# Spreading the four row pairs of the mLSTM mixer over 64 partitions each: selector products on TensorE, or transfers within on-chip memory

## The reference

```python
a_inter = fcum + m0f[:, None, :]
m_t = jnp.maximum(a_inter, jnp.max(dmat, axis=2))
wmat = jnp.exp(dmat - m_t[:, :, None, :])
s = jnp.einsum('bthd,bshd->btsh', qf, kf) * wmat
inter = jnp.exp(a_inter - m_t)
num = inter[..., None] * jnp.einsum('bthd,bhde->bthe', qf, c0f) + jnp.einsum('btsh,bshe->bthe', s, vf)
den = inter * jnp.einsum('bthd,bhd->bth', qf, n0f) + jnp.sum(s, axis=2)
h = num / jnp.maximum(jnp.abs(den), jnp.exp(-m_t))[..., None]
```

## Time and profile before

| | |
|---|---|
| median of 3 runs | 3158.34 us (3158.18 to 3158.46) |
| the profiled execution's own time | 3152.57 us |
| its span, first to last instruction | 3150.7 us |
| mean granted clock of TensorE | 0.947 of full speed |
| TensorE busy | 2927.8 us (93%) |
| VectorE, ScalarE, GpSimd busy | 1327.5, 1120.5, 1446.1 us (42, 36, 46%) |
| mean DMA rate | 83 GB/s |

### The profile page before, as it was taken

The page is one execution under the profiler, slowest core; times in us unless marked ns, Lnnn a source line. Parts: engine busy times, 40 slices in busy tenths (PEclk is TensorE's granted clock), DMA queues, the critical chain, the costliest instruction groups (busy, mean ns, idle before and its releaser), DMA issues.

```text
span 3150.7 us, 43886 instructions
## 1 busy us (share of the span) xinstructions
PE 2927.8 (93%) x18104; PEld 2543.3 (81%) x18104; DVE 1327.5 (42%) x2341; ACT 1120.5 (36%) x1734; POOL 1446.1 (46%) x912
## 2 busy tenths in 40 slices
PE   4768879999999999999999989999999999999998
PEld 3556568787887789898997888778788778999998
DVE  6444246435532455453442344743653242222222
ACT  4322154332332344443223244443233233322222
POOL 2143144345652474445653364434564246455554
PEclk9878689999998999999999999999999899999999
DMA  2111022322221242222222124222222124222332
GB/s 106 39 35 42 25 88 75 94 89 87 81 82 54 83 147 88 88 81 78 83 82 74 55 94 128 88 75 94 87 81 82 49 88 148 88 94 94 90 96 84
DMA packets 80292, 261.26 MB, mean 83 GB/s; under 512 B 10722, under 2 KB 12002, under 8 KB 80096
## 3 DMA queue, kind: packets, MB, share of 16 engines
q1 hardware_dynamic: 63008, 228.04, 23.1%
q10 hardware_dynamic: 17088, 30.43, 2.7%
HBM read 244.90 MB, written 13.54 MB: 82 GB/s over the span
## 4 chain that ended last, share of the span: by engine, by line
PE 81%; DVE 9%; ACT 3%; POOL 3%; issue 2%; ACTq 1%; DMA 1%; SPq 0%; DVEq 0%; POOLq 0%
PE pj L500 23%; PE pj L502 23%; PE pj L501 23%; DVE sl L1482 2%; PE pm L574 2%; PE pm L744 2%; PE pm L838 1%; PE pm L843 1%; POOL w_lo L1371 1%; PE pm L816 1%; PE pm L812 1%; POOL m_lo L1455 1%; DVE sl L1628 1%; ACT w_hi L896 1%; DVE wide L1894 1%
## 5 line engine op out<-in xcount | busy, mean ns | idle before, releaser
L1371 POOL TENSOR_TENSOR w_lo<-w_raw,w_hi 128x1024 fp32r<-128x1024 f32 x428 | 1047.0, 2450 | 1047.2 <-ACT w_hi L896 1047.1
L500 PE MATMUL pj<-hid,w_hi 128*128 128x260 f32 (+1 forms) x1920 | 630.4, 328 | 26.9 <-POOL hid L1448 13.0
L500 PE MATMUL pj<-m_hi,w_hi 128*128 128x260 f32 (+1 forms) x1920 | 623.0, 325 | 10.3 <-POOL m_lo L1455 5.8
L502 PE MATMUL pj<-hid,w_lo 128*128 128x260 f32 (+1 forms) x1920 | 620.7, 323 | 0.0
L502 PE MATMUL pj<-m_hi,w_lo 128*128 128x260 f32 (+1 forms) x1920 | 615.2, 320 | 0.0
L501 PE MATMUL pj<-m_lo,w_hi 128*128 128x260 f32 (+1 forms) x1920 | 614.4, 320 | 0.0
L896 ACT ACTIVATE w_hi<-w_raw 128x1024 fp32r<-128x1024 f32 x428 | 448.4, 1051 | 442.1 <-PE pj L502 408.9
L501 PE MATMUL pj<-hid,w_hi 128*128 128x260 f32 (+1 forms) x1536 | 495.4, 323 | 0.0
L500 PE MATMUL pj<-n_hi,w_hi 128*128 128x260 f32 (+1 forms) x1200 | 395.4, 329 | 30.8 <-DVE n_lo L1523 30.2
L1482 DVE TENSOR_TENSOR res<-res,pj 128x260 f32<-128x260 f32 (+1 forms) x432 | 219.2, 512 | 473.4 <-PE pj L502 471.9
L500 PEld LDWEIGHTS pj<-hid,w_hi 128*128 128x128 f32 x1920 | 367.3, 191 | 62.8 <-POOL hid L1448 14.3
(11 more groups left out here) (298 smaller groups left out, 3483.3 us busy)
## 6 DMA issues: line engine op xcount, KB each, us to landing
w_raw<-in_w SPq DMA_DIRECT2D x428, 512.0 KB, 3.5
out_y<-res ACTq DMA_DIRECT2D x16, 260.0 KB, 4.6
out_y<-res ACTq DMA_DIRECT2D x16, 256.0 KB, 4.6
sl<-in_x ACTq DMA_DIRECT2D x4, 520.0 KB, 5.4
res<-in_x ACTq DMA_DIRECT2D x8, 260.0 KB, 4.8
res<-out_y ACTq DMA_DIRECT2D x8, 260.0 KB, 5.0
res<-in_x SPq DMA_DIRECT2D x4, 512.0 KB, 6.6
res<-out_y ACTq DMA_DIRECT2D x8, 256.0 KB, 4.9
```

The source lines that it names most:

```text
L500: pe.matmul(out, wh, hi[:, k, c0:c1], start=(k == 0), stop=False)
L502: last = pe.matmul(out, wl, hi[:, k, c0:c1], start=False, stop=(k == n - 1))
L1371: pool.tensor_tensor(w_lo[:, j % RAW_BUFS, :], w_raw[:, j % RAW_BUFS, :], w_hi[:, j % HI_BUFS, :].bitcast(F32), ALU.subtract).then_inc(lo_ ...
```

## The change

TensorE's selector products for n = 0 to 3 and ScalarE's copies of them go. In their place ScalarE issues, at the step n = 0 and behind the same wait for do1, eight transfers from `rows8` to `nsp`: for each of the four slots i and each half h, one row is read (a single partition, repeated 64 times) and written to 64 partitions. Their semaphore `bc_ld` reaches 128 per pass when all eight have landed. GpSimd waits for it ahead of the first `qe` of a pass, in place of its wait for the copies; VectorE waits for it ahead of the first update of the state. TensorE's own wait for the copies, ahead of L812, goes.

```diff
@@ -208,7 +208,7 @@
-            elif what in ('rope', 'rot', 'norm1', 'norm2') or what == 'mprep' and x[2] < 4:
+            elif what in ('rope', 'rot', 'norm1', 'norm2'):
...
@@ -787,15 +787,13 @@
             def mprep(x):
                 q, n = x[1:]
-                if n == 4:
-                    pe.wait_ge(hc_sv, NC * (q + 1))
...
+                if n < 4:
                     return
-                at = 64 if n < 2 else 32
-                mix(MIX[x], q, sel[at:at + 4, n % 2 * P:(n % 2 + 1) * P], rows8[at:at + 4, :])
+                pe.wait_ge(hc_sv, NC * (q + 1))
...
@@ -803,7 +801,6 @@
                     if c == 0:
-                        mixed(pe, MIX[('mprep', q, 3)] + len(TILES[q % 2]))
                         for name in ('dq0', 'dq1', 'dk0', 'dk1'):
                             evicted(pe, ('job', q, name))
...
@@ -1198,14 +1195,19 @@
                     act.wait_ge(mm, SHOT[('job', q, 'do1')] + len(TILES[q % 2]))
                     if q % 2:
                         act.dma_start(nflat(4, 2)[:, 0:1024], cs_in[q // 2]).then_inc(cs_ld, 16)
+                    act.wait_ge(rows_a, 3 * q + 3)
+                    tok = TOKENS[q % 2]
+                    for i in range(4):
+                        for h in range(2):
+                            row = (64 if i < 2 else 32) + 2 * (i % 2) + h
+                            act.dma_start(nsp[64 * h:64 * h + 64, i, 0:tok],
+                                          rows8[row:row + 1, 0:tok].unsqueeze(1).to_broadcast([1, 64, tok])).then_inc(bc_ld, 16)
...
                     act.activation(tiny[:, 0:16], pm[:, 3, 0:16], ACT.Copy).then_inc(mp_w, 1)
-                    return
-                take_mix(MIX[x], q, nsp[:, n, :], ACT.Copy)
...
@@ -1426,7 +1428,7 @@
                 if c == 0:
-                    mixed(pool, MIX[('mprep', q, 1)] + len(TILES[q % 2]))
+                    pool.wait_ge(bc_ld, 16 * 8 * (q + 1))
...
@@ -1991,6 +1993,8 @@
                 dve.wait_ge(mc_nt, 2 * g + 2)
+                if c == 0:
+                    dve.wait_ge(bc_ld, 16 * 8 * (q + 1))
```

More of the change, by code:

```diff
@@ L427, in build @@
         nm_a, nm_r, nm_v = sem("nm_a"), sem("nm_r"), sem("nm_v")
-        mp_t, mp_w = sem("mp_t"), sem("mp_w")
+        mp_t, mp_w, bc_ld = sem("mp_t"), sem("mp_w"), sem("bc_ld")
         mc_t, mc_w, mc_s, mc_k, mc_q, mc_nt, mc_d, mc_h, mc_sv = (
@@ L789, in mprep @@
                 q, n = x[1:]
-                if n == 4:
-                    pe.wait_ge(hc_sv, NC * (q + 1))
[L792 to L795, removed]
-                    return
-                at = 64 if n < 2 else 32
-                mix(MIX[x], q, sel[at:at + 4, n % 2 * P:(n % 2 + 1) * P], rows8[at:at + 4, :])
+                if n < 4:
+                    return
+                pe.wait_ge(hc_sv, NC * (q + 1))
+                for j in range(2):
+                    last = pe.matmul(pm[:, 3, j * 8:j * 8 + 8], sel[0:4, j * P:(j + 1) * P],
+                                     rows8[0:4, S0:S0 + DEC], start=True, stop=True)
+                last.then_inc(mp_t, 1)
             def mc(x):
```

## The result

The changed kernel takes 3270.98 us (median of 6 runs, 3264.26 to 3277.34) against 3157.64 us for the kernel before (6 runs): a ratio of 1.0362, with a 95% interval of 1.0346 to 1.0378. It is slower by 113 us; 127 were forecast, and the time lies within the range. The profiled execution took 3270.76 us with a span of 3269.0.

A forecast was written before the change was run, and what follows sets the result against it. TensorE, 81% of the chain, was taken to bound, bare from do1 to first readout. Gaps of 41.9 us (even) and 43.9 (odd), 171.6 in place of 44.9, gave +126.7: 3279.3 profiled, 3285 as median; range 3195 to 3350.

The forecast's parts named there:

- The bare stretch: From do1's last product to the first readout, once per pass: nothing covers it, 44.9 us in all before the change.
- The size of the transfers: Time for the eight row transfers' 1.05 MB per pass: from 2.4 us at 435 GB/s to 38.5 at 27.2 GB/s.
- the narrow end: One source partition feeds no more than one DMA engine's worth, 27.2 GB/s: 38.5 us per even pass, 39.2 odd.
- the paragraph on the port table: Trainium skill, SBUF ports: four neighbouring partitions share one port of some 27.2 GB/s; 19.3 us for each four transfers.
- The row on which the size leaned: Value-cache load into 127 partitions in odd passes, nearest by shape: 520,192 B in up to 31.5 us, at least 16.5 GB/s.
- The sum: Gaps from do1 to first readout: 41.9 us even, 43.9 odd, 171.6 in all in place of 44.9, +126.7.
- The state load's delay: Odd passes, ScalarE's queue: state load L1200 goes ahead of the transfers, 0.35 us to issue and 1.2 for its 512 KB.
- The hand-over: From the transfers' landing to the readout: 1.0 us, made of qe's 0.72 and two hand-overs.
- B: Rival at the row transfers: narrow but twice as wide, gaps 94.0 us in all, +49, 3207 us; chance 0.16.
- C: The forecast itself: narrow row transfers, likeliest 3285 us, by itself 3260 to 3350, rates down to 19 GB/s; chance 0.64.
- D: Rival at the row transfers: half a path, 13.6 GB/s, engines in each other's way, +282, 3440 us; chance 0.06.
- A: Rival at the row transfers: one partition feeds all engines, gaps 28 to 37 us in all, about 3146 us; chance 0.14.

## Why the prediction was right

*The bare stretch.* It was right that nothing covers the four places: +115.1 us of gap became +118.3 of span. The remaining 3 us are of no one place. Before do1 of the first pass, where no instruction differs, the kernel after is already 4.35 us later (334.26 against 329.91), and over the whole program such differences partly cancel. No weights came late either: what the dense products waited for split weights (L500 on `w_lo`) is 6.7 us in both kernels.

*The size of the transfers.* Here the two ends were 2.4 and 38.5 us with a factor of sixteen between, and the narrow end was chosen. It was right: 38.06 us from the first issue to qe in the first pass. The reason given was the single source partition; the two runs with other sources show that it is the source, and the pair on 32 and on 96 shows that it is a path shared by a group, not the partition, as the paragraph on the port table had it.

The row on which the size leaned hit it by luck. The load of 127 rows was near in rate, but it is narrow in another way, which the prediction had allowed for. Here is ScalarE's queue, q10 (packets, MB, share of sixteen engines), in the 12 us from 566 while that load drained before, and in the 34 us from 338 of the kernel after:

```profile
q10 hardware_dynamic: 64, 0.26, 5.7%
...
q10 hardware_dynamic: 599, 0.98, 86.9%
```

The cache load moved 22 GB/s and took 0.057 of sixteen engines, about the time of one. The row transfers moved 29 and kept fourteen engines' worth of time occupied. So the row was a good guide only because about one engine's time and one source path came to nearly the same rate.

*The sum* was too high by 11.6 us (171.6 for the gaps, 160.0 measured). Nearly all of it lies between the first issue and qe: data and fixed part were put at 40.1 us even, and at 40.8 odd with 1.2 more behind the state load; it took 38.06, 38.2, 37.9 and 38.8 in the four passes. The rate was right, 27 GB/s from 338 to 354 and again from 356 to 370. What the sum had wrong is that the second four stand wholly behind the first: in the 2 us from 354 to 356, when one group ended and the next had been issued, 59 GB/s moved; what lies over 27 is worth some 2.4 us (an estimate from these two rates). The state load's delay hardly shows: the gaps of the odd passes exceed the even ones by 0.3 to 1.3 where 2.0 were forecast. The hand-over was put at 1.0 and took 0.78.

*Slips that change nothing.* The 16.5 GB/s of the cache load was to stay for the range, but would have given some 3386 us; the 3350 at which the range ends is 19 GB/s. B, C and D have 0.86 between them, while 0.85 stands for slower. Of the waits on ScalarE's copies in the first pass one lies inside L574's 3.12 us, not two; the other is L812's.

*What was not foreseen.* The prediction took ScalarE's issuing for short once the transfers were on their way, and gave 0.35 to 0.63 us for one. In the first pass they took 0.5 to 6.0, and 27.0 in all; the longest of the run took 7.1. It cost nothing in the changed kernel, since the landing came later still; with the wait halved it became the bound. The 6.80 us of the rope load in the earlier trace rows, issued behind the narrow cache load, was such a held issue, and stood among the rows.

*The rivals.* A (one partition feeds all engines) is excluded by the landing times: engine time was there (a share of 0.87 of sixteen), and it got 27 to 29 GB/s. B is excluded by the 40 us gaps; its picture, two groups read at a time, holds for 2 us of the wait, and for most of it once the groups are on two queues, with 25 to 30 us. D would have shown 80. The clock did as forecast: 0.50 for 7 us behind the wait. The fourth and the eighth transfer landed 17.2 us apart (355.8 and 373.1) where some 20 were named; the overlap of the two groups is in that too.

## What to carry to other kernels

To spread a row over many partitions by transfers, don't read it from one on-chip partition: 64 copies of 2 KB came at 27 to 29 GB/s, while the same copies out of device memory landed some four times as fast. Before replacing work on an engine by a transfer, ask when its source is ready and its target free: the gaps fell from 44.9 us to 38.7 with the engine's work gone and the rows in device memory, and to 22.5 only when a free target let half of them go ahead of the critical stretch. A busy share of the DMA engines is no rate: read the GB/s beside it. And a transfer that drains slowly holds up the engine that issues the next one; count what stands behind it in that queue.

## What the runs showed of the hardware

- Transfers out of partitions 64 to 67, and then out of 32 to 35, moved 27 GB/s with sixteen engines at a busy share of 0.88 to 0.89, and 59 GB/s in the 2 us in which both groups were read. With the second group on another queue it was 52 GB/s; with the second group at 96 to 99 it stayed at 27.
- A load into 127 partitions moved 22 GB/s and took 0.057 of the sixteen engines' time: the same rate, narrowed in another way.
- Issuing one such row transfer on ScalarE's queue took 0.55 us for the first and up to 5.97 for a later one of the first pass, 27.0 for eight; from many partitions, or from device memory, 0.62 each.
- A busy share of DMA engines near 1 went with 435, 222, 52, 29 and 27 GB/s in different stretches (shares 1.08, 1.00, 0.93, 0.87 and 0.90). The share says that engines are occupied, not that they move much.
